# The last quarter of the MLP's input projection as seven block products in place of eight, on one Trainium2 core

## What is computed

```python
x = x + rms_norm(y, post_norm_mix[l])
h = rms_norm(x, pre_norm_mlp[l])
y = jnp.square(jax.nn.relu(h @ w_mlp_in[l])) @ w_mlp_out[l]
x = x + rms_norm(y, post_norm_mlp[l])
```

## Time and profile before

| | us |
|---|---|
| median of 3 runs | 750.17 (750.15 to 750.27) |
| the profiled execution, its own time | 749.34 |
| its span in the trace | 747.6 |
| PE busy | 740.2 (99% of the span), 4168 matmuls |
| DVE, ACT, POOL busy | 435.5, 389.5, 324.9 |

### The profile page before, as it was taken

How to read it: one execution, slowest core, us unless ns; L and a number is a source line. 1 busy time by engine, 2 the same in 40 slices (tenths; PEclk the granted TensorE clock), 3 DMA queues, 4 the chain that set the end, 5 groups by cost and what they waited for, 6 DMA issues and landing times.

```text
span 747.6 us, 11913 instructions
## 1 busy us (share of the span) xinstructions
PE 740.2 (99%) x4168; PEld 607.8 (81%) x4168; DVE 435.5 (58%) x651; ACT 389.5 (52%) x632; POOL 324.9 (43%) x296
## 2 busy tenths in 40 slices
PE   9999999999999999999999999999999999999996
PEld 7788778888877878788888988888888888888885
DVE  5897899980454545444983512221221777778795
ACT  6657842268554365635655733333332655555671
POOL 2348894435454754574536466546545000000002
PEclk9999999999999999999999999999999999999999
DMA  9436224456476597276650279979978575554652
GB/s 330 113 87 211 57 71 114 127 128 150 132 171 156 169 198 197 64 160 202 210 185 28 85 233 274 238 227 294 237 227 216 159 228 194 198 184 154 220 174 114
DMA packets 86302, 129.22 MB, mean 173 GB/s; under 512 B 6096, under 2 KB 45168, under 8 KB 86256
## 3 DMA queue, kind: packets, MB, share of 16 engines
q1 hardware_dynamic: 76384, 109.47, 45.8%
q0 software_dynamic: 9536, 18.88, 14.8%
q10 hardware_dynamic: 336, 0.28, 0.1%
HBM read 126.49 MB, written 39.86 MB: 223 GB/s over the span
## 4 chain that ended last, share of the span: by engine, by line
PE 93%; POOL 3%; ACT 2%; DVE 1%; DMA 0%; issue 0%; SPq 0%; POOLq 0%; ACTq 0%; DVEq 0%
PE bank L767 28%; PE bank L768 27%; PE bank L769 27%; POOL rsq L2167 2%; PE bank L1014 1%; PE bank L1037 1%; PE bank L1024 1%; POOL w_lo L2173 1%; PE bank L978 1%; PE bank L788 1%; PE bank L942 1%; PE bank L794 1%; PE bank L989 1%; PE bank L797 0%; PE bank L1076 0%; DMA raw<-in_w_in 0%
## 5 line engine op out<-in xcount | busy, mean ns | idle before, releaser
L2173 POOL TENSOR_TENSOR w_lo<-raw,w_hi 128x512 fp32r<-128x512 f32 x169 | 219.4, 1308 | 232.7 <-ACT w_hi L1229 230.7
L1229 ACT ACTIVATE w_hi<-raw 128x512 fp32r<-128x512 f32 (+2 forms) x214 | 145.1, 684 | 154.6 <-PE bank L769 126.5
L767 PE MATMUL bank<-h_hi,w_hi 128*128 128x512 f32 (+1 forms) x528 | 208.6, 395 | 0.2
L768 PE MATMUL bank<-h_lo,w_hi 128*128 128x512 f32 (+1 forms) x528 | 204.2, 387 | 0.0
L769 PE MATMUL bank<-h_hi,w_lo 128*128 128x512 f32 (+1 forms) x528 | 204.1, 387 | 0.0
L767 PEld LDWEIGHTS bank<-h_hi,w_hi 128*128 128x128 f32 x528 | 99.2, 188 | 26.1 <-issue 5.1
L769 PEld LDWEIGHTS bank<-h_hi,w_lo 128*128 128x128 f32 x528 | 99.2, 188 | 20.5
L768 PEld LDWEIGHTS bank<-h_lo,w_hi 128*128 128x128 f32 x528 | 99.3, 188 | 18.6
L1638 DVE SCALAR_TENSOR_TENSOR relu_sb<-bank,rs_row 128x512 f32<-128x512 f32 x32 | 20.6, 686 | 126.5 <-PE bank L769 114.8
L2311 POOL TENSOR_SCALAR ssh<-ssy 128x1 f32<-128x1 f32 x4 | 1.0, 238 | 151.6 <-ACT junk L1609 151.6
L767 PE MATMUL bank<-w_hi,a_hi 128*128 128x512 f32 x120 | 46.8, 390 | 0.0
(11 more groups left out here) (327 smaller groups left out, 1268.0 us busy)
## 6 DMA issues: line engine op xcount, KB each, us to landing
raw<-in_w_in SPq DMA_DIRECT2D x87, 256.0 KB, 2.9
raw<-in_w_mlp_in SPq DMA_DIRECT2D x62, 256.0 KB, 4.9
t_sum<-in_w_mlp_out POOLq DMA_DIRECT2D x12, 1024.0 KB, 10.7
raw<-in_w_mlp_out SPq DMA_DIRECT2D x26, 256.0 KB, 3.1
raw<-t_sum SPq DMA_DIRECT2D x26, 256.0 KB, 3.2
v_sum<-in_w_mlp_out SPq DMA_DIRECT2D x4, 1024.0 KB, 6.5
t_sum<-in_w_mlp_out SPq DMA_DIRECT2D x4, 1024.0 KB, 7.2
v_sum<-in_w_mlp_out POOLq DMA_DIRECT2D x4, 1024.0 KB, 11.4
```

The source lines that it names most:

```text
L767: pe.matmul(o, s_hi, m_hi, start=start, stop=False, skip_group_check=True)
L768: pe.matmul(o, s_hi, m_lo, start=False, stop=False, skip_group_check=True)
L1229: return a.activation(o, i_, ACT.Copy, scale=scale)
L2173: g.tensor_tensor(w_lo[:, slot, :], raw[:, slot, :], w_hi[:, slot, :].bitcast(F32), ALU.subtract).then_inc(lo_ready, 1)
```

## The change

- The first 12 groups of the MLP's input (`G_PLAIN`) stay. The last 1024 columns (two halves of `F_HALF = 512`) are done in two steps (`STEPS_IN`) by seven block products in place of eight: K in halves of 512, features in two halves, tokens in halves of 256. A step has 14 units (`PER_STEP`), two per product; a unit is 128 x 512 weights as before and takes 2 x 2 x 3 = 12 matmuls, of 256 tokens each.
- Four weight sums for it, `u_sum`, of 512 x 512, one chunk each (`CHUNKS = 1`, 1 MB), are made in DRAM by copies at units 10, 14, 36 and 43 and accumulating DMAs two units later. Two copies for the mixer's output move from units 48 and 52 to 51 and 55, two of `SUM_AT` from 61 and 65 to 62 and 66.
- `SUM_IN` loses its last two chunks, (3, 2) and (3, 3); SP now copies them in `one(2)` and `one(3)` of the output. The sums' last chunks are cut otherwise in the rows of `w_mlp_out` (`w2_late`).
- The activations' block sums are made during the groups i = 2 and 3: DVE adds hi and lo again (4 x 128x1024), makes four sums, ACT their hi parts, DVE the lo parts. They lie where x_res and pn_mlp were: SP stores x_res to DRAM (4 x 512 KB) in groups 2 and 3, POOL loads it and pn_mlp back after unit `U_M1` and the last sums.
- In the steps raw units use a ring of eight buffers; POOL makes 4 of 14 lo parts, DVE 10. Each step has ten sums of 128x256 from banks on DVE, two relus of 128x256 and two of 128x768, two copies of 128x256 on ACT, four squares.
- At the hand-over ACT does its squares (now of two groups, four operations) after `w_split(6, 2)`, and DVE does two sums of 128x256 before `w_low(3)` and the two relus of 128x768 before `w_low(6, 2)`, in place of two relus of 128x512.

```diff
+G_PLAIN = 12
+F_HALF = (FF - G_PLAIN * 256) // 2
+U_S = U_OUT + 4 * G_PLAIN
+STEPS_IN = F_HALF // 256
+PER_STEP = 14
+RING = 8
+CHUNKS = F_HALF // 512
+U_M1 = U_S + STEPS_IN * PER_STEP
-OUT_SUM_AT = {48: 0, 52: 1, 60: 2, 87: 3}
+OUT_SUM_AT = {51: 0, 55: 1, 60: 2, 87: 3}
-SUM_AT = {61: (0, 0), 65: (1, 0), 73: (2, 0), 74: (0, 1), 78: (1, 1), 86: (2, 1)}
+SUM_AT = {62: (0, 0), 66: (1, 0), 73: (2, 0), 74: (0, 1), 78: (1, 1), 86: (2, 1)}
+IN_SUM_AT = {10: (0, 0), 14: (1, 0), 36: (2, 0), 43: (3, 0)}
-SUM_IN = {2: (0, 2), 3: (0, 3), 4: (3, 0), 5: (3, 1), 7: (2, 2), 8: (2, 3), 9: (1, 2), 10: (1, 3), 12: (3, 2), 13: (3, 3)}
+SUM_IN = {2: (0, 2), 3: (0, 3), 4: (3, 0), 5: (3, 1), 7: (2, 2), 8: (2, 3), 9: (1, 2), 10: (1, 3)}
+IN_PRODUCTS = ("q1", "q6", "q5", "q2", "q7", "q3", "q4")
+LOW_POOL = (1, 3, 7, 11)
...
# SP, groups 2 and 3
+                if g in (2, 3) and j % 2:
...
+                    sp_.dma_start(x2_copy[t], x_res[:, t, :]).then_inc(copied_out, 16)
# SP, the steps
+        for s in range(STEPS_IN):
+            for v in range(PER_STEP):
+                u = U_S + PER_STEP * s + v
+                if v >= RING - RAW or s:
+                    sp_.wait_ge(*low_of(u - RING))
+                dst = raw_of(u).rearrange("p (k c) -> p k c", k=2)
+                sp_.dma_start(dst, in_source(s, v)).then_inc(raw_signal(u)[0], 16)
# SP, the output
+        for i in (2, 3):
             one(i)
+            if i == 2:
+                sp_.wait_ge(*added(2, N_SUM))
+            sp_.dma_start(*t_copy(3, i)).then_inc(t_copied[3 if i == 2 else 1], 16)
# PE
+            for half in range(2):
+                u = U_S + PER_STEP * s + 2 * IN_PRODUCTS.index(name) + half
+                pe.wait_ge(*low_of(u))
+                for kk in range(2):
+                    for e in range(2):
+                        c = slice(kk * 256 + e * P, kk * 256 + e * P + P)
+                        x_ = three(bank[IN_BANK[name] + e][:, 0:256], w_hi[:, u % SPL, c], w_lo[:, u % SPL, c],
+                                   *in_operand(name, 2 * half + kk), name in ("q1", "q6", "q5") and half + kk == 0,
+                                   name in ("q2", "q4", "q3") and half + kk == 2)
+                x_.then_inc(unit_done, 1)
# ACT, hand-over
         a_split(1, 1, slice(0, 4))
-        square_group(NI - 1, 1)
         w_split(6, 2, 16)
+        for e in range(2):
+            square_in(STEPS_IN - 1, e)
# DVE, hand-over
-        relu(NI - 1, ms=(2, 3))
+        w_low(2, 1, 3)
+        v.wait_ge(unit_done, U_M1)
+        for e in range(2):
+            c21(STEPS_IN - 1, e)
         w_low(3, 1, 4)
         w_low(4, 2, 6)
         a_low(1, 1, slice(0, 4), 2)
+        for e in range(2):
+            relu_in(STEPS_IN - 1, e)
         w_low(6, 2, 8)
# POOL, after the input
+        add_sum(3, 2)
+        g.wait_ge(*copied(1, N_SUM + 1))
+        g.dma_start(*t_add(3, 3), accum_op=ALU.add).then_inc(t_added[3], 16)
+        g.wait_ge(unit_done, U_M1)
+        for t in range(NT):
+            g.dma_start(x_res[:, t, :], x2_copy[t]).then_inc(late_in, 16)
+        g.dma_start(pn_mlp[:], post_norm_mlp[0].partition_broadcast(P)).then_inc(late_in, 16)
```

More of the change, by code:

```diff
@@ L442, in program @@
     pn_in = sem("pn_in")
+    late_in = sem("late_in")
     ssy_ready = sem("ssy_ready")
@@ L715, in one, with two @@
                     sp_.wait_ge(part_lo, i * 8 + (s + 2 - 8))
-                part(s, one_source(i, s))
-        def two(i, before):
+                part(s, one_source(i, s, late))
+        def two(i, before, late=False):
             for s in range(6):
@@ new lines, in split_in, with mlp_in_last @@
+        def split_in(u):
+            a.wait_ge(*raw_signal(u))
+            a.wait_ge(unit_done, u - 3)
+            copy(w_hi[:, u % 4, :], raw_of(u)).then_inc(hi_ready, 1)
+        def mlp_in_last(i):
+            for j in range(8):
+                u = U_OUT + LEAD + 8 * i + j
+                if u < U_S:
+                    split(None, u % 4, 16 * loads(u), u - 3)
+                else:
+                    split_in(u)
+                if j in (3, 7):
+                    square_group(i, j // 4)
```

377 lines of the change are left out of this document (305 added, 72 removed).

## The result

The changed kernel takes **760.46 us** (median of 4 runs, 758.87 to 763.46) against 750.16 for the kernel before on the same chip: a ratio of 1.0144, interval 1.0117 to 1.0171. The forecast was 748.7 with a range up to 751.3, so it is wrong in sign and by 11.8 us. The profiled execution took 763.46 us with a span of 761.7, which is 14.1 longer than the 747.6 of before, and 3 us more than the median: this kernel's own runs differ by more than those of before do (4.6 us from lowest to highest, against 0.8).

What follows compares the result with a forecast made beforehand. PE was taken as the bound, busy 99% of the span. Profiled: 749.34 - 3.2 (matmuls) + 0.05 (supply) + 1.7 (hand-over stall) = 747.9; for the median 750.17 - 1.45 = 748.7 us, range 746.9 to 751.3.

Steps and rivals of the forecast that it cites:

- The matmuls: In the two steps: 336 matmuls of 256 columns take 40.3 us in place of 43.5, saving 3.2 us.
- Supply in the steps: In the two steps: ACT, DVE, POOL and loads keep double pace; cost 0.05 us, ends 0 and 0.3.
- rival of pace: In the steps: DVE and POOL exclude each other more or buffers free late; 2.8 us lost, time 751.5; chance 0.07.
- Moved and added transfers: Early sums, x_res stores, moved copies and activations' block sums, all ahead of the steps: cost 0, ends 0 and 0.5 us.
- a new wait before 415 us from the sums in units 10 to 47: Listed sign that the forecast is wrong: PE waiting there because of the four new sums, which were costed at nothing.
- The four new sums: Units 10 to 47: copies and adds delay SP's loads and add POOL issues of 1.2 us, PE waits for nothing; cost 0.
- The blocks of the activations: Two groups of 21.8 us each: 12 DVE operations and 4 ACT copies end before the next relu is due; cost 0.
- The stores of x_res: Groups 2 and 3: four stores add 2 MB and come before the busiest stretch; cost 0.
- The hand-over: From steps to output, at one(1): ACT and DVE late with a_low(2), PE stalls 1.7 us, ends 0 and 2.4; no-stall rival 0.25.
- Late transfers: In one(2) and one(3): two 1 MB copies, two accumulations, 2.5 MB of reloads fit the loads' 5 us slack; cost 0.
- the collision: Rival, one(2) to one(6): late sums and reloads delay the output's loads; PE loses 3 us (751.7) or 5 (753.7); chance 0.13.
- The chances: Forecast 0.50, no stall 0.25, late collision 0.13, steps behind 0.07, no saving 0.05; faster 0.45, within 0.43, slower 0.12.

Runs made afterwards that it cites:

- experiment 2: Changed kernel without the four early sums of w_mlp_in blocks (copies, adds and waits left out; same-size blocks read instead): 756.47 us, ratio 1.0081.
- 7: Changed kernel with the first early add moved behind unit 15 and the second early sum to units 47 and 50, nothing left out: 755.39 us, ratio 1.0078.
- experiment 5: Changed kernel without the making of the four input blocks (DVE's twelve block operations, ACT's four ts_hi): 758.12 us, ratio 1.0112.
- experiment 1: Changed kernel without the four x_res stores and ACT's wait for them; input x read back instead: 762.36 us, ratio 1.0149.
- 12: 11 with only ACT's squares moved behind one(1), a_hi(2) and a_lo(2) earlier, raw_c loaded earlier, POOL's wo_lo waiting for DVE's low parts: 747.46 us, ratio 0.9958.
- 13: 12 with the four x_res stores one group earlier, in groups 1 and 2: 746.91 us, ratio 0.9957.
- 6: Changed kernel with the first five block sums of the plain phase moved to groups 1 to 5, nothing left out: 762.73 us, ratio 1.0174.
- 10: Changed kernel with squares and relus behind one(1), last two sums as four halves behind one(2) to one(5), x_res read back in four steps: 754.36 us, ratio 1.0062.
- 9: Changed kernel with DVE's block operations spread two per group over groups 5 to 10, behind POOL's split; ts_hi in groups 8 and 9: 759.43 us, ratio 1.0134.
- 11: Changed kernel with the edits of 7, 9 and 10 together: 751.16 us, ratio 1.0015.

## Why the prediction was wrong, step by step

- **The matmuls: right.** 336 in 40.31 us against 40.3, and 3.1 us less span once nothing else was in the way. The estimate that the prediction worked out from the Trainium skill (TensorE: Matmul & The Clock Gate, Back-to-back issue gap), a saving of 4.8 us, does not hold here: the matmuls of 256 columns stand 120.0 ns apart where it has 109.2.
- **Supply in the steps: right.** 0.05 us forecast, none lost; the clock was 1.00 and no rival of pace showed.
- **Moved and added transfers: the step that failed**, in three terms, all costed at 0 (0 to 0.5), where the profiled run lost 9.8 us. The prediction named the sign, "a new wait before 415 us from the sums in units 10 to 47", and it came. *The four new sums* cost 2.8 us by the time x_res is loaded (347.8 against 344.9) and 4 to 5 in the time (experiments 2 and 7). The step counted landing times and one more POOL issue of 1.2 us, but not what that issue does to the order of POOL's splits against DVE. The row that could have warned stood in the prediction (1.54 in place of 0.42 us) and was used for the steps only. *The blocks of the activations* "even in alternation with POOL they end before the next relu is due": they did, roughly, but the test was the wrong one. It asked whether DVE is done in time and not what POOL's splits, loads and adds do meanwhile. That cost up to 5.6 us in the profiled run (1.0 + 3.0 + 1.6 of clock), none when left out (experiment 5), and at most 0.5 us of waits with the blocks made but the early sums out or moved (2 and 7): by these single profiles it took both. One more microsecond went at 389, where DVE's h_lo and w_lo took 1.7 us beside POOL's wo_lo (0.7 each in experiment 2); what brings the two together there is open. *The stores of x_res* cost nothing by themselves (experiment 1) and something between 0 and 3 us in the company of sums and block making (profiles of 12 and 13).
- **The hand-over: mechanism right, size a little off.** Stall forecast 1.7 (0 to 2.4), measured 2.2 with PE's releaser a_lo (for "the semaphore and weight load", which the prediction put at 0.25, the trace shows 0.13 from the end of a_lo to PE's start) and the four squares just ahead of the late split, as said. ACT, after:

```profile
600.50 1.06 ACT L1402 ACTIVATE wb_hi<-raw_c 128x1024 fp32r<-128x1024 f32 x1 [2.20 <-DMA raw_c<-v_sum]
601.47 2.18 ACT L1712 ACTIVATE act_end<-relu_sb 128x512 f32<-128x512 f32 x4
603.56 1.99 ACT L1402 ACTIVATE w_hi<-raw 128x1024 fp32r<-128x1024 f32 x2
```

  The difference is raw_c. ACT's split of it ended at t + 6.0 (t = 595.57) where I had 4.6: SP issued the load 0.5 us later, behind two parts of one(1), and it landed after 3.8 us in place of 3.0. ACT's next split began at t + 8.0 where I had 7.4, a smaller delay, since in my count ACT had to wait for the relus anyway.
- **Late transfers: the rival came true.** "Cost 0 in the forecast", chance 0.13 for the collision at "3 (up to 5) us". It took 2.7 us of stall and 1.6 of clock, at 652, in the place named. What the rival left out is the clock.
- **The chances** followed from the zeros: a slower end of 0.12 rested on the late collision and a part of "steps behind". Five added pieces of work, each costed at nothing because a cover was seen, should have had a rival of their own, that some of the covers give way. They did: mended one at a time the places gave from a loss of 2.3 us (6) to a gain of 6.1 (10) and moved stalls about, mended together 13.5 (760.46 to 746.91). That company makes them worse is seen in the profiles of the plain groups (2, 5 and 7; one profile each), not in the times, where the gains of 7, 9 and 10 add up to more than 11 brought.

## What to carry to other kernels

Work added to an engine that is idle half the time was not free here, where that engine and another one shut each other out of SBUF: cost it by what the other one's next deadline is, and look for the row in which both ran together. When a change makes several covered additions around one saving, mend them together before judging it: here each repair alone left the kernel slower than before, most of them within the scatter, and together they turned 1.4% slower into 0.4% faster. In this kernel it paid to put a DMA issue of POOL where POOL has nothing urgent behind it (7, and with it 11 to 13); putting DVE's block operations behind POOL's urgent split showed no gain of its own (9).
